# Second feed-forward: quarter sums by accumulating transfers, and another order of the seven products

## What is computed

```python
def _sqrelu_mlp(h, w1, w2):
    return jnp.square(jax.nn.relu(h @ w1)) @ w2

    h2 = _modulate(_rmsnorm(x, norm2_g), sh2, sc2)
    x = x + g2 * _sqrelu_mlp(h2, w_ff1, w_ff2)
```

## Time and profile before

| | |
|---|---|
| median of 3 runs | 1660.47 us (1659.97 to 1660.49) |
| profiled execution | 1660.74 us |
| its span | 1659.0 us (1.74 us lie around it) |
| mean granted clock of TensorE | 0.999 of full speed |
| TensorE busy | 1627.6 us (98%) |
| VectorE busy | 1110.5 us (67%) |
| ScalarE busy | 763.0 us (46%) |
| GpSimd busy | 150.0 us (9%) |
| moved by DMA | 172.89 MB, mean 104 GB/s |

### The profile page before, as it was taken

How to read it: one execution, slowest core, us unless ns; L and a number is a source line. 1 busy time by engine, 2 the same in 40 slices (tenths; PEclk the granted TensorE clock), 3 DMA queues, 4 the chain that set the end, 5 groups by cost and what they waited for, 6 DMA issues and landing times. The chain is left out here.

```text
span 1659.0 us, 31156 instructions
## 1 busy us (share of the span) xinstructions
PE 1627.6 (98%) x13194; PEld 1301.0 (78%) x13194; DVE 1110.5 (67%) x1579; ACT 763.0 (46%) x1179; POOL 150.0 (9%) x155
## 2 busy tenths in 40 slices
PE   8999999999999999999999999999999999999997
PEld 6666777777767888888888788886578888998987
DVE  6857689888757477676665772364986656775734
ACT  5444555545255443132323553337776544453523
POOL 0000000000000200001111000031100000414101
PEclk9999999999999999999999999999999999999999
DMA  6212231112145343546563232320102233232321
GB/s 227 87 52 71 79 126 42 41 41 92 42 166 190 119 157 135 175 142 237 189 218 108 78 107 77 110 94 18 28 2 79 87 105 101 87 116 79 125 91 51
DMA packets 51323, 172.89 MB, mean 104 GB/s; under 512 B 6128, under 2 KB 9328, under 8 KB 50416
## 3 DMA queue, kind: packets, MB, share of 16 engines
q1 hardware_dynamic: 41456, 134.71, 24.0%
q0 software_dynamic: 9728, 36.18, 6.5%
HBM read 160.64 MB, written 8.39 MB: 102 GB/s over the span
## 5 line engine op out<-in xcount | busy, mean ns | idle before, releaser
L419 PE MATMUL pair<-h_hi,w_hi 128*128 128x512 f32 (+1 forms) x976 | 379.4, 389 | 4.0 <-DVE h_lo L851 1.5
L466 DVE TENSOR_TENSOR w_lo<-w_raw,w_hi 128x1024 fp32r<-128x1024 f32 (+1 forms) x240 | 280.0, 1172 | 142.9 <-ACT w_hi L444 142.8
L421 PE MATMUL pair<-h_hi,w_lo 128*128 128x512 f32 (+1 forms) x976 | 370.2, 379 | 0.0
L420 PE MATMUL pair<-h_lo,w_hi 128*128 128x512 f32 (+1 forms) x976 | 370.1, 379 | 0.0
L444 ACT CAST w_hi<-w_raw 128x1024 fp32r<-128x1024 f32 (+1 forms) x240 | 224.0, 940 | 219.3 <-PE pair L421 201.9
L419 PEld LDWEIGHTS pair<-h_hi,w_hi 128*128 128x128 f32 x976 | 183.6, 188 | 54.4 <-issue 16.2
L420 PEld LDWEIGHTS pair<-h_lo,w_hi 128*128 128x128 f32 x976 | 183.8, 188 | 35.0 <-issue 2.6
L421 PEld LDWEIGHTS pair<-h_hi,w_lo 128*128 128x128 f32 x976 | 183.6, 188 | 35.1
L419 PE MATMUL pair<-ff_f_hi,w_hi 128*128 128x512 f32 (+1 forms) x536 | 204.2, 381 | 0.6 <-DVE w_lo L466 0.6
L420 PE MATMUL pair<-ff_f_lo,w_hi 128*128 128x512 f32 (+1 forms) x536 | 203.5, 380 | 0.0
L421 PE MATMUL pair<-ff_f_hi,w_lo 128*128 128x512 f32 (+1 forms) x536 | 203.5, 380 | 0.0
(11 more groups left out here) (506 smaller groups left out, 2821.1 us busy)
## 6 DMA issues: line engine op xcount, KB each, us to landing
w_raw<-in_w_ff SPq DMA_DIRECT2D x128, 512.0 KB, 3.5
mod_w<-in_w_mod POOLq DMA_DIRECT2D x48, 512.0 KB, 3.7
w_raw<-in_w_in SPq DMA_DIRECT2D x22, 512.0 KB, 3.4
w_raw<-in_w_gate SPq DMA_DIRECT2D x16, 512.0 KB, 3.5
w_raw<-in_w_out SPq DMA_DIRECT2D x16, 512.0 KB, 3.5
w_raw<-in_w_rwkv SPq DMA_DIRECT2D x15, 512.0 KB, 3.4
w_raw<-in_w_da SPq DMA_DIRECT2D x12, 512.0 KB, 4.8
w_raw<-in_w_ple_gate SPq DMA_DIRECT2D x8, 512.0 KB, 3.5
```

The costliest lines, as they stand in the source:

```text
L419: nc.tensor.matmul(out, w_hi, x_hi, start=(k == 0), stop=False)
L420: nc.tensor.matmul(out, w_hi, x_lo, start=False, stop=False)
L421: last = nc.tensor.matmul(out, w_lo, x_hi, start=False, stop=(k == kt - 1))
L466: nc.vector.tensor_tensor(lo[:, slot, cols], source, hi[:, slot, cols].bitcast(F32), ALU.subtract).then_inc(pr.lo_made, 1)
```

## The change

The four sums are made in place in w_raw by DMAs issued from GpSimd that add a quarter read again from DRAM to what is in the tile (`accum_op=ALU.add`), 128 x 512 values or 256 KB each. Onto a21, which becomes s1 = a21 + a22, then s2 = s1 + a11, then s4 = s2 + a12, one after the other, each after the split of the one before; and onto a11, which becomes s3 = a11 + a21 after its own split. As these only add, s2, s3 and s4 have other signs than before, so t1 to t3 and one relu get other signs as well. A chain of three transfers uses one of two semaphores by turns. The chain's first transfer of the next pair is issued behind the last of this one.

The order of the products is s1, a11, a12, s2, s3, a22, s4. The product of s1 ("y"), the fifth in the joins, has a bank of its own (6) in even pairs and bank 2 of the four turning banks in odd pairs. ScalarE copies the product of a11 after the second unit. TensorE waits for the copy ahead of the fifth unit ("w1"), and for the join of the pair two back ahead of y. A slot's first tile is free after unit 4 (s3), the second after unit 6 (s4). The 4th "down" job behind a group of pairs waits for the last pair's third join.

```diff
@@ Program
     def raw_free(self, w):
-        if (w, 5) in self.split_no:
-            return self.split_no[w, 5]
-        return self.split_no[(w - 1, 6) if (w - 1, 6) in self.split_no else w]
+        if (w, PairedUps.LAST_OF_FIRST) in self.split_no:
+            return self.split_no[w, PairedUps.LAST_OF_FIRST]
+        last = (w - 1, PairedUps.LAST_OF_SECOND)
+        return self.split_no[last if last in self.split_no else w]
@@ PairedUps
-    UNITS = (("a11", "b11", "y0"), ("s2", "t2", "x1"), ("a12", "b21", "x0"), ("s3", "t3", "w0"), ("s1", "t1", "y1"), ("s4", "b22", "z0"), ("a22", "t4", "z1"))
-    FIRST, JOIN, NEXT, SPREAD, LAST = 0, 2, 3, 4, 6
+    UNITS = (("s1", "t1", "y"), ("a11", "b11", "w0"), ("a12", "b21", "x0"), ("s2", "t2", "x1"), ("s3", "t3", "w1"), ("a22", "t4", "z1"), ("s4", "b22", "z0"))
+    COPY, JOIN, SPREAD, LAST = 1, 3, 4, 6
+    LAST_OF_FIRST, LAST_OF_SECOND = 4, 6
+    SPARE = 2
...
-    def bank(self, name):
+    def bank(self, name, Q):
+        if name == "y":
+            return self.pr.bank[self.SPARE if Q % 2 else 6][:, 0:TC]
         col = TC * int(name[1])
-        return self.pr.bank[4 + "wxyz".index(name[0])][:, col:col + TC]
+        return self.pr.bank[{"w": 4, "x": 5, "z": 7}[name[0]]][:, col:col + TC]
...
+        added = lambda n: (self.chain[Q % 2], 16 * (3 * (Q // 2) + n))
+        a11, a21 = first[:, 0:512], second[:, 0:512]
...
+               "s1": (a21, added(1)), "s2": (a21, added(2)), "s4": (a21, added(3)), "s3": (a11, (self.third[Q % 2], 16 * (Q // 2 + 1)))}
...
     def before(self, pe, Q, i):
         bank = self.UNITS[i][2]
-        if bank == "y1":
+        if bank == "w1":
             pe.wait_ge(self.copied, Q + 1)
-        elif Q and bank in ("w0", "x1", "y0", "z0"):
-            pe.wait_ge(self.joined, 4 * (Q - 1) + {"w0": 2, "x1": 1, "y0": 3, "z0": 4}[bank])
+        elif bank == "y":
+            if Q % 4 == 1:
+                pe.wait_ge(self.ff.added, KT * (self.group(Q) - 1))
+            if Q > 1:
+                pe.wait_ge(self.joined, 4 * (Q - 2) + 3)
+        elif bank in ("w0", "x0", "z1") and Q:
+            pe.wait_ge(self.joined, 4 * (Q - 1) + {"w0": 2, "x0": 1, "z1": 4}[bank])
...
     def act(self, act, Q, i, bank, done):
-        if i == self.FIRST:
+        if i == self.COPY:
...
-        if i == 1 and Q % 4:
+        if i == 2 and Q % 4:
             self.positives(act, Q - 1)
-        if i in (3, 4) and Q % 4:
-            self.high(act, Q - 1, i - 3)
+        if i in (4, 5) and Q % 4:
+            self.high(act, Q - 1, i - 4)
...
-            self.pr.nc.scalar.activation(part, part, ACT.Relu).then_inc(self.positive, 1)
+            self.pr.nc.scalar.activation(part, part, ACT.Relu, scale=(1.0, -1.0)[t]).then_inc(self.positive, 1)
...
     def dve(self, dve, Q, i, bank, done):
-        if i in (4, 5) and Q % 4:
-            self.low(dve, Q - 1, i - 4)
+        if i in (5, 6) and Q % 4:
+            self.low(dve, Q - 1, i - 5)
...
-        if i == self.NEXT:
+        if i == self.SPREAD:
             dve.wait_ge(self.joined, 4 * Q + 1)
             nc.vector.tensor_tensor(c[:, 2, :], bank, c[:, 1, :], ALU.add).then_inc(self.joined, 1)
-        if i == self.SPREAD:
             dve.wait_ge(self.joined, 4 * Q + 2)
-            nc.vector.tensor_tensor(c[:, 1:4:2, :], bank.unsqueeze(1).to_broadcast([P, 2, TC]), c[:, 1:3, :], ALU.add).then_inc(self.joined, 1)
+            fifth = self.bank("y", Q)
+            nc.vector.tensor_tensor(c[:, 1:4:2, :], fifth.unsqueeze(1).to_broadcast([P, 2, TC]), c[:, 1:3, :], ALU.add).then_inc(self.joined, 1)
...
-    def weights(self, pool, Q):
...
+    def split(self, pool, Q, name):
+        source = [source for source, _, _ in self.UNITS].index(name)
+        pool.wait_ge(self.pr.lo_made, self.pr.split_no[self.pairs[Q], source])
+
+    def add(self, pool, Q, n, name):
+        w = self.pairs[Q] + 1
+        pool.dma_start(self.pr.raw[:, w % RAW_SLOTS, 0:512], self.quarter(Q, name), accum_op=ALU.add).then_inc(self.chain[Q % 2], 16)
+
+    def begin(self, pool, Q):
+        pool.wait_ge(*self.pr.landed(self.pairs[Q] + 1))
+        self.add(pool, Q, 1, "a22")
+
+    def add_third(self, pool, Q):
+        pool.dma_start(self.pr.raw[:, self.pairs[Q] % RAW_SLOTS, 0:512], self.quarter(Q, "a21"), accum_op=ALU.add)\
+            .then_inc(self.third[Q % 2], 16)
 
     def pool(self, pool):
         for Q in range(len(self.pairs)):
-            self.weights(pool, Q)
+            if Q % 4 == 0:
+                self.begin(pool, Q)
+            self.split(pool, Q, "s1")
+            self.add(pool, Q, 2, "a11")
+            self.split(pool, Q, "a11")
+            self.add_third(pool, Q)
+            self.split(pool, Q, "s2")
+            self.add(pool, Q, 3, "a12")
+            if Q % 4 < 3:
+                self.begin(pool, Q + 1)
@@ FeedForward.before
+        if self.paired and kind == "down" and self.paired.first <= g + 1 < FF_GROUPS and j == 3:
+            pe.wait_ge(self.paired.joined, 4 * self.paired.number(g + 1, 3) + 3)
@@ SecondUp.difference
-        nc.vector.tensor_tensor(d[t][:, :, :], one, other, ALU.subtract).then_inc(self.turned_raw, 1)
+        if t in (0, 2):
+            one, other = ((y[0][:, :, early], y[0][:, :, late]), (y[1][:, :, late], y[0][:, :, late]))[t // 2]
+            nc.vector.tensor_tensor(d[t][:, :, :], one, other, ALU.subtract).then_inc(self.turned_raw, 1)
+        else:
+            other = y[1][:, :, late if t == 1 else early]
+            nc.vector.scalar_tensor_tensor(d[t][:, :, :], d[t - 1 if t == 1 else 1][:, :, :], -1.0, other, ALU.mult, ALU.subtract)\
+                .then_inc(self.turned_raw, 1)
@@ SecondUp.dve, at n == 0
-            nc.vector.tensor_tensor(self.shift_step, half[:, 4:8], half[:, 0:4], ALU.subtract).then_inc(self.turned_shift, 1)
+            nc.vector.tensor_tensor(self.shift_step[:, 0:4], half[:, 4:8], half[:, 0:4], ALU.subtract).then_inc(self.turned_shift, 1)
+            nc.vector.tensor_scalar(self.shift_step[:, 4:8], half[:, 4:8], -1.0, None, ALU.mult).then_inc(self.turned_shift, 1)
```

More of the change, by code:

```diff
@@ L2856, with __init__ @@
 class PairedUps:
-    UNITS = (("a11", "b11", "y0"), ("s2", "t2", "x1"), ("a12", "b21", "x0"), ("s3", "t3", "w0"), ("s1", "t1", "y1"), ("s4", "b22", "z0"), ("a22", "t4", "z1"))
-    FIRST, JOIN, NEXT, SPREAD, LAST = 0, 2, 3, 4, 6
-    def __init__(self, pr, name, first, parts, turned_hi, turned_lo, sums, copy, turned_ready):
+    UNITS = (("s1", "t1", "y"), ("a11", "b11", "w0"), ("a12", "b21", "x0"), ("s2", "t2", "x1"), ("s3", "t3", "w1"), ("a22", "t4", "z1"), ("s4", "b22", "z0"))
+    COPY, JOIN, SPREAD, LAST = 1, 3, 4, 6
+    LAST_OF_FIRST, LAST_OF_SECOND = 4, 6
+    SPARE = 2
+    def __init__(self, pr, name, first, parts, turned_hi, turned_lo, copy, turned_ready):
         self.first = first
-        self.pr, self.sums, self.copy, self.turned_ready = pr, sums, copy, turned_ready
+        self.pr, self.copy, self.turned_ready = pr, copy, turned_ready
         x_hi, x_lo = parts
@@ L2872, in __init__ @@
         self.pairs = []
-        self.summed, self.copied, self.joined, self.positive, self.squared = (
-            pr.sem(f"{name}_{k}") for k in ("w_sum", "copied", "joined", "positive", "squared"))
-    def bank(self, name):
+        self.chain, self.third = ([pr.sem(f"{name}_{k}{i}") for i in range(2)] for k in ("w_chain", "w_third"))
+        self.copied, self.joined, self.positive, self.squared = (pr.sem(f"{name}_{k}") for k in ("copied", "joined", "positive", "squared"))
+    def bank(self, name, Q):
+        if name == "y":
+            return self.pr.bank[self.SPARE if Q % 2 else 6][:, 0:TC]
         col = TC * int(name[1])
-        return self.pr.bank[4 + "wxyz".index(name[0])][:, col:col + TC]
+        return self.pr.bank[{"w": 4, "x": 5, "z": 7}[name[0]]][:, col:col + TC]
     def job(self, w, Q, i):
@@ L2885, in job @@
         first, second = pr.raw[:, w % RAW_SLOTS, :], pr.raw[:, (w + 1) % RAW_SLOTS, :]
-        raw = {"a11": (first[:, 0:512], pr.landed(w)), "a12": (first[:, 512:1024], pr.landed(w)), "a22": (second[:, 512:1024], pr.landed(w + 1)),
-               "s1": (self.sums[0], (self.summed, 4 * Q + 1)), "s2": (self.sums[1], (self.summed, 4 * Q + 2)),
-               "s3": (second[:, 0:512], (self.summed, 4 * Q + 3)), "s4": (self.sums[2], (self.summed, 4 * Q + 4))}
+        added = lambda n: (self.chain[Q % 2], 16 * (3 * (Q // 2) + n))
+        a11, a21 = first[:, 0:512], second[:, 0:512]
+        raw = {"a11": (a11, pr.landed(w)), "a12": (first[:, 512:1024], pr.landed(w)), "a22": (second[:, 512:1024], pr.landed(w + 1)),
+               "s1": (a21, added(1)), "s2": (a21, added(2)), "s4": (a21, added(3)), "s3": (a11, (self.third[Q % 2], 16 * (Q // 2 + 1)))}
         pr.units[w, i] = raw[source]
-        return Job(w, self.moving[moving], TC, unit=i, bank=self.bank(bank))
+        return Job(w, self.moving[moving], TC, unit=i, bank=self.bank(bank, Q))
     def number(self, g, q):
@@ L2972, in low @@
```

(21 more changed lines are left out.)

15 lines of the change are left out of this document (7 added, 8 removed).

## The result

The median of four runs with the change is **1681.43 us** (1680.02 to 1682.38), against 1660.48 us (1659.97 to 1660.92) for four runs of the kernel before on the same chip: ratio **1.0126 [1.0108, 1.0143]**, slower by 21 us. The profiled execution took 1681.28 us with a span of 1679.5 us, 20.5 us longer than the span before.

What follows compares the result with a forecast made beforehand. TensorE, busy 98% of the span, was taken as the bound. Stalls of 4.5 us less 2.18 us won gave +2.3 us on 1660.74, 1663.1; the median, 0.27 us lower, 1662.8 us; range 1658.0 to 1677.

Steps and rivals of the forecast that it cites:

- the ring: Pair-to-pair loop of two transfer landings, two splits and an issue: 11.35 us a turn against TensorE's pace of 10.08 us.
- The ceiling of 2.18 us: TensorE's idle time in both groups of pairs, credited whole to the change and the most it could win.
- Comes at no cost: Claim that scalar_tensor_tensor differences, a tiny tensor_scalar, the fourth "down" job's wait and SP's loads are covered, adding nothing.
- L: An accumulating transfer's time from issue to landing, taken as 3.7 us from plain 512 KB loads on GpSimd's queue.
- second: Chain transfer making s2, issued after s1 is split; priced at 3.7 us from issue to landing.
- begin: Chain transfer making s1, issued for the next pair right behind this pair's final one; priced at 3.7 us to landing.
- last: Chain transfer making s4, issued after s2 is split; priced at 3.7 us from issue to landing.
- The issue: GpSimd's time to issue one transfer, taken as 0.54 us; much more would make the prediction wrong altogether.
- The due time at the fifth unit: s4 must land within 4.8 us of the pair's start, since the copy TensorE awaits stands behind its cast.
- The handover to "down": After a group's final pair, ScalarE's and VectorE's work delays the first "down" tile: 0.7 us more stall a group.
- the transfers become the bound: Rival, chance 0.27: four accumulating transfers and two loads fill 0.96 of the transfer engines, landing in 5 us; 1678 us.
- The chain is hidden: Rival, chance 0.30: transfers land in 3.2 us or less, no stall stays in the pairs; 1658.3 us.

Runs made afterwards that it cites:

- e4: Kernel after with its adding transfers undone: the four sums made on GpSimd as before, new product order and two banks kept; 1657.78 us, ratio 0.9985.
- e5: New product order with the sums on GpSimd, but one bank instead of two for the fifth product; 1659.87 us, 0.9997 of the kernel before.
- e2: Kernel after with plain copies in place of the adding transfers, same sizes, queue and waits, sums not formed; 1664.27 us, ratio 1.0025.
- e3: Kernel after without the transfer that makes s3, a11 used unsummed in its product; 1682.79 us, ratio 1.0133.
- e6: Kernel after with the next pair's first transfer issued ahead of the wait for s2's split, and no transfer for s3; 1678.13 us, ratio 1.0105.
- e9: Kernel after with the next pair's first transfer issued early and no transfer for s4, whose product uses s2's tile; 1662.48 us, ratio 1.0016.
- e7: Kernel after with each adding transfer over 256 of its 512 columns, half of each sum not formed; 1669.35 us, ratio 1.0052.

## Why the prediction was wrong, point by point

The prediction said 1662.8 us in a range of 1658 to 1677; it is 1681.4. The first place where TensorE waits, what it waits for there and the sign were right; the length of the ring was not.

- **The ceiling of 2.18 us was right**, and e4 takes all of it, but the credit was put on two things together, short subtractions and the second bank. e4 and e5 show that, in the new order, the bank is what counts: subtractions stay long in e4, as its row of 1.78 us shows.
- **"Comes at no cost" held.** Between the groups and behind them, where the wait at the fourth "down" job stands, the time is the same to 0.1 us. The scalar_tensor_tensor differences (L3500) come ahead of the first group, which begins at 1432.49 and, with the same differences, at 1433.53 in e4, against 1433.50 before. As for SP's loads, TensorE's waits in the pairs and at the handovers go to the copy and the join, all but 1.0 us in three waits for w_lo.
- **The step that failed is L, one value for every transfer.** It was taken as 3.7 us, from plain 512 KB loads. In the turn from 1453.71, *second* took 4.62 us and *begin*, right behind *last* in one queue, 6.57 us. e2 shows that the adding is what is dear: a plain copy of 256 KB lands in 3.1 us there. The page "Collectives: The Full Stack" of the Trainium skill (section on the bandwidth ceiling), cited for two source reads and a free add, fits what the engines spend (the rows under the rivals below). It does not carry over to the landing: the 3.2 us estimated from the page "DMA: Bandwidth & Descriptors" of the Trainium skill (section on one SWDGE transfer) is below every landing of an adding transfer in the kernel after, 3.9 us at the least.
- **The issue was taken as 0.54 us; it lasts 0.86 us**, which the prediction had named as a thing that would make it wrong. It is no term of its own in the ring, though: the next issue starts 0.54 us behind the first (1459.97 to 1460.51), so the 0.55 us of the formula stands, and what the longer issue costs lies within the landings, which are counted from the issue's start.
- **The ring as worked out was 2L + 3.95 = 11.35 us; it is 15.08 us.** The differences are 0.92 us for *second* and 2.87 for *begin*: 3.79, less 0.06 us by which the splits (1.64 and 1.71 us, predicted as 1.7) and the issue are shorter, is the 3.73 measured. So the formula stood and its main term was mis-sized, most of all for the transfer that is second in line. "The *begin* waits in one queue right behind *last*" stands in the prediction as an argument, but without a price.
- **The due time at the fifth unit was right.** The copy stands behind s4's cast and releases TensorE six times, for 9.2 us in all. The handover to "down" cost 0.33 us of wait and 0.48 us of time where 0.7 was said.
- **A second due time was missed.** TensorE also waits 7.4 us, ahead of the second unit, for the join L2971; a stall at another unit than the fifth was the other sign that the prediction had named against itself. VectorE's timeline of the kernel after shows what stands ahead of it:

```profile
1452.73 0.69 DVE L467 TENSOR_TENSOR w_lo<-w_raw,w_hi 128x512 fp32r<-128x512 f32 x1 [1.79 <-ACT w_hi L445]
1455.33 0.69 DVE L467 TENSOR_TENSOR w_lo<-w_raw,w_hi 128x512 fp32r<-128x512 f32 x1 [1.91 <-ACT w_hi L445]
1455.94 0.69 DVE L2968 TENSOR_TENSOR ff_sq<-pair,ff_copy 128x512 f32<-128x512 f32 x1
1456.54 0.68 DVE L467 TENSOR_TENSOR w_lo<-w_raw,w_hi 128x512 fp32r<-128x512 f32 x1
1457.14 0.42 DVE L2971 TENSOR_TENSOR ff_sq<-pair,ff_sq 128x256 f32<-128x256 f32 x1
```

  The subtraction at 1452.73 is that of pair 2's s1, late with its transfer; the casts of the units behind it, and so their subtractions at 1455.33 and 1456.54, come later still, and the joins of pair 1, whose products are long done, stand between them. A late s1 is thus paid not at its own unit (which starts without a wait at 1454.88) but at the one behind it, at 1457.61, where TensorE asks for the join of the pair before.
- **The clock was not in the sum.** In the fourth pair matmuls start 0.21 us apart (1474.49 to 1474.70) where a unit of 12 in 1.44 us has them 0.12 apart, and the granted clock of the windows falls to 0.71 and 0.66, between the 2.4 and the 1.2 GHz level. Before it TensorE had stood still four times in this group, for 1.13 to 2.74 us each (the last of them, 1.74 us, at 1472.69). The two units from 1472.69 take 4.46 us in place of 2.88, 1.58 us more; in two groups that is some 3.2 us.
- **The rivals.** Nearest in time was "the transfers become the bound", 1678 us with a chance of 0.27. Its L of 5 us is near the mean of the ring's two landings, 5.6 us. Its reason did not come true: the share is 0.64 and not 0.96, and e3, e6 and e9 differ by up to 20 us with equal bytes. That transfers in flight together stretch each other may still be so, and lie within those landings. "The chain is hidden" needed 3.2 us; the adding transfers took 3.9 us and more. Yet the price that the bound rival put on the engines was right, as the queues of the kernel after show from 1430 to 1590 us (packets, MB, share of 16 engines; then the issues):

```profile
q0 software_dynamic: 4176, 7.60, 30.3%
q1 hardware_dynamic: 3906, 14.23, 27.4%
...
w_raw<-in_w_ff SPq DMA_DIRECT2D x28, 512.0 KB, 4.1
w_raw<-in_w_ff POOLq DMA_DIRECT2D x29, 256.0 KB, 4.3
```

  An adding transfer of 256 KB holds the engines for 0.303 x 160 / 29 = 1.67 us, a load of 512 KB for 0.274 x 160 / 28 = 1.57 us. At TensorE's pace a pair would fill (4 x 1.67 + 2 x 1.57) / 10.08 = 0.97 of them. The ring is so slow that it never comes to that; a faster ring with four such transfers a pair would meet this limit next, by this estimate, which no run tried.

Not settled: how much a load of SP's beside an adding transfer lengthens its landing, and what makes the clock fall in some stretches with stalls and not in others. For the first, the trace of the kernel after has six *begin* right behind a *last*: the two with no load of SP's issued within 4 us (at 1430.09 and 1525.47) landed after 5.5 and 5.4 us, the four with one within 2 us after 6.4 to 7.8. That points to 1 us or more of the ring, but no run varies the loads alone.

## What to carry to other kernels

Where a change puts transfers into a chain from one unit of work to the next, write the ring down, with each transfer at its own price, dearer for an adding one and for one behind another in its queue, and compare it with the pace of the engine that bounds the kernel; free share on the transfer engines does not show it. Look at every in-order queue through which the chain's data pass, for a consumer that takes its items in a fixed order can close the ring where the queue that issues them does not. And when a change has several parts, the plain one (here a second bank) may hold all of the gain: try the parts one by one.

## What the runs showed of the hardware that was not expected

- An accumulating transfer takes GpSimd 0.86 us to issue, at 512 and at 256 columns alike (e7), against 0.54 us for a plain one between the same places (e2).
- With nothing ahead of it in its queue, it lands in 3.9 to 4.6 us for 256 KB in most turns of the kernel after, and in 5.8 and 5.2 us for the *second* of pair 1 of each group (issued at 1437.55 and 1532.97), with two loads of SP's in flight and the s3 transfer 1.2 us behind it. The plain copy has a median of 3.1 us, a plain load of 512 KB from the same queue 3.7 us. Right behind another one it takes 5.2 to 7.8 us.
- In the fourth pair of the kernel after, stalls of 1.98, 1.13, 2.74 and 1.74 us were followed by a granted clock of 0.71 and 0.66 in the windows from 1472.60 to 1478.00. That makes a chain's stall dearer than its waits add up to. In e2, with waits of 0.32 to 1.08 us, the granted clock of both groups stayed at 1.00.
